# RWKV scan: one 128-row product per head for output and for state, identity and old state added on TensorE

## What is computed

```python
def step(s, inp):
    w_t, k_t, v_t, kk_t, a_t = inp[:5]
    sa = jnp.einsum('bhvk,bhk->bhv', s, kk_t)
    s = (s * w_t[:, :, None, :] - sa[..., None] * (kk_t * a_t)[:, :, None, :]
         + v_t[..., None] * k_t[:, :, None, :])
    if not want_out:
        return s, None
    return s, jnp.einsum('bhvk,bhk->bhv', s, inp[5])
```

## Time and profile before

| | |
|---|---|
| time, median of 3 runs | 2241.44 us (2238.55 to 2246.93) |
| span of the profiled execution | 2243.0 us, of which no time outside the span is given |
| busy in it: PE, DVE, ACT, POOL | 2044.1, 1366.9, 786.2, 275.6 us |
| the scan phase | from 973.9 us; the next phase's chain of work begins at 1277.4 us |
| granted clock of TensorE, mean | 0.954 of 2.4 GHz |

### The profile page before, as it was taken

One profiled execution on the slowest core, in us unless ns is written; L12 is line 12 of the kernel. 1 busy time (PEld: TensorE's weight loads), 2 busy tenths in 40 slices (PEclk: granted clock), 3 DMA queues, 4 the chain that ended last, 5 costly groups with the idle time before them and its releaser, 6 DMA issues. The chain is left out here.

```text
span 2243.0 us, 38706 instructions
## 1 busy us (share of the span) xinstructions
PE 2044.1 (91%) x16787; PEld 1683.7 (75%) x16787; DVE 1366.9 (61%) x1287; ACT 786.2 (35%) x858; POOL 275.6 (12%) x135
## 2 busy tenths in 40 slices
PE   7679999999899989966677799989999999999997
PEld 3258888888678876656666688778888888888886
DVE  3465666665438547758888678366565656554444
ACT  1231112113062225524433365344343434333333
POOL 0242213123104214301000020000000000000000
PEclk9589999999899999988999899999999999999998
DMA  9989888886264368977444287535555555555552
GB/s 327 349 273 335 309 310 301 310 316 193 90 170 106 85 186 262 302 194 189 86 88 88 52 205 269 204 120 188 187 187 187 187 188 188 185 206 188 191 199 98
DMA packets 406153, 454.18 MB, mean 202 GB/s; under 512 B 107551, under 2 KB 356751, under 8 KB 388735
## 3 DMA queue, kind: packets, MB, share of 16 engines
q1 hardware_dynamic: 398400, 441.04, 62.0%
q10 hardware_dynamic: 7614, 11.10, 1.3%
HBM read 413.89 MB, written 38.22 MB: 202 GB/s over the span
## 5 line engine op out<-in xcount | busy, mean ns | idle before, releaser
L215 DVE TENSOR_TENSOR f_w_lo<-t_w_raw,f_w_hi 128x2048 fp32r<-128x2048 f32 x132 | 302.2, 2290 | 308.1 <-ACT f_w_hi L209 308.1
L270 PE MATMUL pf<-h,f_w_hi 128*128 128x512 f32 x1320 | 463.9, 395 | 0.0
L209 ACT ACTIVATE f_w_hi<-t_w_raw 128x2048 fp32r<-128x2048 f32 x132 | 253.2, 1918 | 446.8 <-PE pf L270 283.6
L269 PE MATMUL pf<-h,f_w_lo 128*128 128x256 f32 x1320 | 367.4, 278 | 0.3 <-DVE h L2603 0.3
L270 PEld LDWEIGHTS pf<-h,f_w_hi 128*128 128x128 f32 x1320 | 247.6, 188 | 54.3
L269 PEld LDWEIGHTS pf<-h,f_w_lo 128*128 128x128 f32 x1320 | 248.3, 188 | 4.6 <-DVE h L2603 0.6
L209 ACT ACTIVATE p_w_hi<-h_w_raw 128x2048 fp32r<-128x2048 f32 (+1 forms) x52 | 96.4, 1901 | 340.6 <-DVE stage L726 252.2
L261 PE MATMUL p_in<-h,p_w_lo 128*128 128x512 f32 (+1 forms) x512 | 199.3, 389 | 0.0
L259 PE MATMUL p_in<-h,p_w_hi 128*128 128x512 f32 (+1 forms) x512 | 199.3, 389 | 0.0
L260 PE MATMUL p_in<-h,p_w_hi 128*128 128x512 f32 (+1 forms) x512 | 199.3, 389 | 0.0
L2799 PE MATMUL d_out<-f_w_hi,hid 128*128 128x512 f32 x704 | 178.7, 394 | 6.2 <-DVE f_w_lo L215 6.2
(11 more groups left out here) (417 smaller groups left out, 3362.9 us busy)
## 6 DMA issues: line engine op xcount, KB each, us to landing
h_of_x<-in_ada_w SPq DMA_DIRECT2D x64, 1024.0 KB, 5.1
h_w_raw<-in_w_in SPq DMA_DIRECT2D x51, 1024.0 KB, 7.5
t_w_raw<-in_ffn_w_gate SPq DMA_DIRECT2D x44, 1024.0 KB, 5.1
t_w_raw<-in_ffn_w_up SPq DMA_DIRECT2D x44, 1024.0 KB, 5.1
t_w_raw<-in_ffn_w_down SPq DMA_DIRECT2D x44, 1024.0 KB, 4.9
h_w_raw<-in_ada_w SPq DMA_DIRECT2D x32, 1024.0 KB, 8.8
gate_w<-in_w_in SPq DMA_DIRECT2D x32, 1024.0 KB, 6.2
t_w_raw<-in_w_out SPq DMA_DIRECT2D x16, 1024.0 KB, 5.7
```

The source lines that it names most:

```text
L209: act.activation(self.hi[:, m % self.S, 0:w], self.raw[:, s, 0:w], ACT.Copy)\
L215: eng.tensor_tensor(self.lo[:, m % self.S, 0:w], self.raw[:, s, 0:w], b32(self.hi[:, m % self.S, 0:w]), ALU.subtract)\
L269: pe.matmul(hi, wl, x[:, 0, k, :], start=False, stop=False)
L270: return pe.matmul(both, wh, x[:, :, k, :], start=False, stop=last)
```

## The change

It pairs operands so that a product over 128 rows does what two over 64 did. `uv` holds, for each head, u on one half of the partitions and v on the other; which half is which depends on the parity of j. `r12` holds `r1` and `r2`, `st12` holds `s1t` and `s2t` in the same way, and `s12` (rate and key side by side, in an order that depends on the parity) takes the place of `ldr`'s rows 1 and 2; to have it so, `phase_rwkv_pre` writes keys and rates, and v, of odd pairs in swapped places. Outputs of `uv` are copied from PSUM in two parts, by parity.

Two additions go to TensorE: `inverse` is preceded by a product of identities in f32r (`eye_r`, `eyes_r`), after which `xt` is only 0.5 x PSUM, a copy on ScalarE; and `u_step` puts the old state into PSUM by a product with `eye`, so that VectorE's `state` is the multiplication by `e_end` alone.

```diff
@@ phase_rwkv_pre, store
-                    sp.dma_start(shared_d.rearrange("p (a j) t -> p a j t", a=2)[:, :, j, :], sh[:, j % 3])\
+                    apart = PAIRS + 1 - 2 * b
+                    sp.dma_start(shared_d[:, j:j + apart + 1:apart, :], sh[:, j % 3])\
...
@@ run
-                go("flips2", now)
+                go("halve", lev)
                 if not early:
                     go("prepare", ahead)
                     go("forward", ahead)
-                go("halve", lev)
@@ SyncE
                     if c:
-                        for n in ("q1", "b", "s2tr"):
+                        sp.wait_ge(sm("b", d), c)
+                    sp.dma_start(ld[d][:], dir_d[d, :, 0:U8, at:at + C]).then_inc(sm("in", d), 16)
+                    if c:
+                        for n in ("q1", "strn"):
                             sp.wait_ge(sm(n, d), c)
-                    sp.dma_start(ldr[d][:].rearrange("p a u t -> p (a u) t"), dir_d[d, :, :, at:at + C])\
-                      .then_inc(sm("in", d), 16)
+                    for n in range(2):
+                        sp.dma_start(s12[d][:, :, n, :], dir_d[d, :, U8 + U8 * n:2 * U8 + U8 * n, at:at + C])\
+                          .then_inc(sm("in_s12", d), 16)
@@ VectorE, scores
-                    dve.tensor_tensor(quads(r1[d][:]), narrow(pb[d]), mask(INCL, d), ALU.mult)\
-                       .then_inc(sm("r1", d), 1)
+                    dve.tensor_tensor(r12[d][:], whole(pb[d]), masks[:, d, INCL, :].unsqueeze(1)
+                                      .broadcast_to([P, 2 * U8, C]), ALU.mult).then_inc(sm("r12", d), 1)
@@ VectorE, halve and state
-                    dve.scalar_tensor_tensor(out=quads(xt[d][:]), in0=narrow(pa[d]), scalar=0.5,
-                                             in1=quads(half_eye[:]), op0=ALU.mult, op1=ALU.add)\
-                       .then_inc(sm("inverse", d), 1)
...
-                    dve.tensor_tensor(by_parity(S[d][:]), by_parity(S[d][:]), narrow(pa[d], 1), ALU.add).then_inc(sm("sadd", d), 1)
-                    dve.wait_ge(sm("sadd", d), c + 1)
                     dve.wait_ge(sm("e_end", d), c + 1)
-                    dve.tensor_tensor(S[d][:], S[d][:], e_end[d][:].unsqueeze(2).broadcast_to([P, U8, C]), ALU.mult)\
-                       .then_inc(sm("S", d), 1)
+                    dve.tensor_tensor(by_parity(S[d][:]), narrow(pa[d], 1), e_end[d][:].rearrange("p (u b) -> p b u", b=2)
+                                      .unsqueeze(3).broadcast_to([P, 2, U8 // 2, C]), ALU.mult).then_inc(sm("S", d), 1)
@@ ScalarE
-                    act.activation(quads(vt[d][:]), narrow(pb[d]), ACT.Copy).then_inc(sm("vt", d), 1)
+                    for b in range(2):
+                        act.activation(own_blocks(uv[d], b)[HEAD[1 - b]].rearrange("p h u c -> p u h c"),
+                                       pb[d][HEAD[1 - b], 0:BANK].rearrange("p (u h c) -> p u h c", h=2, c=C), ACT.Copy).then_inc(sm("vt", d), 1)
...
+                    act.activation(st12[d][:], whole(pa[d]), ACT.Copy).then_inc(sm("st12", d), 1)
+
+                def halve(c, d):
+                    act.wait_ge(sm("k", d), c + 1)
+                    act.activation(quads(xt[d][:]), narrow(pa[d]), ACT.Copy, scale=0.5).then_inc(sm("inverse", d), 1)
...
-                    act.activation(quads(u[d][:]), narrow(pa[d]), ACT.Copy).then_inc(sm("uc", d), 1)
+                    for b in range(2):
+                        act.activation(own_blocks(uv[d], b)[HEAD[b]], narrow(pa[d])[HEAD[b]], ACT.Copy).then_inc(sm("uc", d), 1)
@@ TensorE, scores3, tokens, flips
+                    pe.wait_ge(sm("first", d), c + 1)
...
+                        last = pe.matmul(by_block(pb[d], j, h), s12[d][HEAD[h], j].rearrange("p a c -> p (a c)"),
+                                         feat(q12[d][:, :, 1, :], j, h), start=True, stop=True)
...
-                        pe.wait_ge(sm("r1", d), c - 3)
-                    turn_all(pb, kkv[d][:, 1], d).then_inc(sm("vtr", d), 1)
+                        pe.wait_ge(sm("r12", d), c - 3)
...
+                    for j in range(U8):
+                        last = pe.transpose(pa[d][:, j * P:(j + 1) * P], s12[d][:, j].rearrange("p a c -> p (a c)"), eye[:])
+                    last.then_inc(sm("strn", d), 1)
@@ TensorE, grow level 0
-                        pe.wait_ge(sm("s1t", d), c + 1)
+                        pe.wait_ge(sm("st12", d), c + 1)
@@ TensorE, inverse and u_step
+                    for b in range(2):
+                        pe.matmul(pa[d][:, b * BANK:b * BANK + BANK // 2], eye_r[:],
+                                  eyes_r[:].rearrange("p u c -> p (u c)"), start=True, stop=False, skip_group_check=True)
...
+                    goes_on = c != LAST
+                    if goes_on:
+                        for b in range(2):
+                            at = b * BANK + BANK // 2
+                            pe.matmul(pa[d][:, at:at + BANK // 2], eye[:],
+                                      S[d][:].rearrange("p (u b) c -> p b u c", b=2)[:, b], start=True, stop=False,
+                                      skip_group_check=True)
@@ TensorE, output and state
-                        pe.matmul(by_feature(pb[d], j, h), flip(vt[d], j, h), tok(r2[d], j, h), start=False, stop=False, skip_group_check=True)
-                    pe.wait_ge(sm("uc", d), c + 1)
-                    for j, h in UNITS:
-                        last = pe.matmul(by_feature(pb[d], j, h), tok(u[d], j, h), tok(r1[d], j, h), start=False, stop=True, skip_group_check=True)
+                        at = block_of(j, h)
+                        last = pe.matmul(by_feature(pb[d], j, h), uv[d][:, at, :], r12[d][:, at, :], start=False, stop=True,
+                                         skip_group_check=True)
...
+                    for j, h in UNITS:
+                        last = pe.matmul(by_feature(pa[d], j, h, 1), st12[d][:, 2 * j + h, :], uv[d][:, block_of(j, h), :],
+                                         start=False, stop=True, skip_group_check=True)
```

146 lines of the change are left out of this document (66 added, 80 removed).

## The result

The changed kernel takes 2246.48 us (median of 10 runs, 2242.30 to 2252.39) against 2241.48 us before (10 runs on the same chip); the ratio is 1.0029 with a 95% interval of 1.0015 to 1.0042. It got slower, by 5 us between the medians and 6.5 us by the ratio, where 8.6 us less were forecast. The profiled execution has a span of 2246.1 us, so it stands for the median.

What follows compares the result with a forecast made beforehand. VectorE (nearly without holes in context half steps) and, in latent ones, TensorE's instruction supply were taken to bound the kernel; 4.4 (context) + 3.2 (latent) + 1.0 (start) = 8.6 us off 2241.4 gave 2232.8 us, range 2217 to 2249.

Steps and rivals of the forecast that it cites:

- the sum for the latent half step: Latent half step: 18.1 us of chain plus 0.5 us remaining of the supply gaps, 18.6 us instead of 19.0.
- +1.4 us: Latent half step without instruction supply: +0.9 at level 2, +1.2 at level 0, -0.7 for the state addition gone.
- (2): Latent half step: scores3 doubles from 0.5 to 0.93 us plus a 0.1 switch, r12 waits; 0.7 us of level 0's delay.
- VectorE's work, 20 us less: Whole kernel: halving (10.8 us) and state addition (9.5 us) leave VectorE, 20.3 us of busy time.
- Identity ahead of u, +0.9 on level 2: Latent half step: the product of identity and old state takes 1.1 us between level 1 and u; level 2 costs 0.9 more.
- Level 0, 1.2 us later, of which the copies of v make 0.5: Latent half step: level 0 returns 1.2 us later, 0.7 from scores3 and r12, 0.5 from the copies of v.
- Supply: Latent half: instructions arrive one packet per about 4.0 us; 16.1 us per half step against 18, 24 to 25 packets against 27.
- Context half steps, 0.55 us shorter: Context half step: halving gives 0.3 us, state addition 0.5, identity product costs 0.25; 4.4 us over 8.
- The start, 1.0 us: Start of the scan: the smaller load ld lands ahead of s12, gaining 1.0 of the first scan's 1.6 us wait.
- The second one: Rival: the chain grows and the supply gives nothing back, gaps staying as long; +5.8 us, 2247 us, chance 0.15.
- The third: Rival: 128-row products don't overlap, so state and output take up to 3.7 us each; 2280 us, chance 0.10.
- The first: Rival: VectorE's time comes off whole, a gain of 20 us or more; 2220 us, chance 0.20.

Runs made afterwards that it cites:

- e1: Changed kernel with each 64x128 product of scores3 made two 64x64 products on alternating quarters of the array; 2238.95 us, ratio 1.0001 to the kernel before.
- e4: Changed kernel with scores3 in quarters, flips ahead of the tokens, and the carried-state products ahead of level 1; 2230.92 us, ratio 0.9974 to the kernel before.
- e5: Changed kernel with the addition of the old state back on VectorE and the products of identity and state gone; 2247.10 us, ratio 1.0024 to the kernel before.
- e6: Changed kernel with halving and identity again one VectorE operation, f32r identity products and ScalarE's halving gone; 2243.82 us, ratio 1.0018 to the kernel before.
- e3: Changed kernel with the two products of identity and old state moved two steps earlier, behind the sum for rhs; 2242.96 us, ratio 1.0016 to the kernel before.
- e14: Kernel of e13 with the two copies of v also made one, leaving out more of state and output; 2247.85 us, ratio 1.0034 to the kernel before.
- e2: Changed kernel with the flips of the sources and their copy ahead of the tokens and the copies of v; 2247.43 us, ratio 1.0038 to the kernel before.
- e13: Changed kernel with ScalarE's two copies of u made one of 128 partitions, leaving out part of the result; 2247.26 us, ratio 1.0028 to the kernel before.
- e7: Kernel before the change without the r2 by v output products and s2 by v state products, 32 fewer per latent half step; 2221.09 us, ratio 0.9908.
- e9_early_inverse: Kernel of e4 with VectorE's transposes into cross ahead of r12 and the inverse with its halving ahead of the tokens; 2230.84 us, ratio 0.9958.
- e8: Changed kernel with VectorE's two transposes into cross ahead of r12 instead of behind it; 2246.63 us, ratio 1.0022 to the kernel before.
- e11: Kernel before the change with the products that e7 removes kept, but cut to 2 of their 64 columns; 2241.94 us, ratio 1.0010.

## Why the prediction was wrong

**The step that failed** is the sum for the latent half step: "With 18.1 us of chain and 16.1 us of supply I expect 0.5 us of it to remain: 18.6 us". It measured 20.4 us. That is the larger part of the error; a context half step missed by 0.7 us (16.7 for 16.0). Two terms of the latent sum failed.

The first is the chain, "+1.4 us". A clean latent half step of the changed kernel has 14.3 us of VectorE's work and waits of 1.54, 1.49 and 1.35 us, 18.7 us in sum and not 18.1. The mis-sized part is (2), `scores3` "0.5 to 0.93, one switch of 0.1": it went from 0.50 us (1214.47 to 1214.96 before the change) to 1.93, 0.9 us more than I had. e1 brings it to 0.99 and takes 0.8 us off the wait for `r12`.

The second is what remains beside the chain. TensorE's gaps did fall to 0.5 us per half step, but the half step lies 1.7 us above the clean one. Over the six that is 10 us. Of these, 3.5 are waits for `r12` and level 2 behind groups that ran at the granted clock of 0.50 in part or whole (2.90, 2.44 and 2.57 us instead of 1.35, 1.54 and 1.54), 2.7 are such waits where records came late (2.83, 2.07 and 2.08 us), and 2.2 are waits for `first`. I subtracted the relief from the half step as if gaps and TensorE's work were apart. A gap in which instructions arrive can be TensorE's slack; here TensorE filled it with longer work. For this reading stand e4, in which the shorter work brings 10.4 us of gaps back, and the busy time, 13.9 before and 16.4 us after per latent half step. That it is the whole reason isn't shown.

The sentence "TensorE's time is thus unchanged; what falls is the count" holds for the products it speaks of. At full clock the output took 0.47 + 0.47 us and the state, whose two groups are interleaved, 0.93 before the change, 1.87 together; after it 0.95 to 0.98 and 1.03 to 1.06. What the prediction never did is to add up TensorE's time over the whole half step. These lines make up the 14.7 us by which it grew over six:

| us busy | before | after |
|---|---|---|
| scores2 | 9.4 | 5.2 |
| scores3 | 5.1 | 13.3 |
| identity by S | none | 7.7 |
| f32r identity of the inverse | none | 2.9 |

(Busy times of lines can't be added where groups are interleaved, as in the state before the change, so I compare output and state by their starts.)

Point by point:

- *scores3, "0.5 to 0.93, one switch of 0.1".* Measured 1.93 us. I counted 64x128 as two tiles at the pace of a row with two tiles; the timeline gives 1.93 us for 32 records, 0.060 each, and its weight loads of 128 columns last 188 ns where those of 64 last 135. What e1 changes here is worth 6 to 7.5 us of the whole.
- *VectorE's work, 20 us less.* In the profiles 24.1 us less (1366.9 to 1342.8). As traded it was worth nothing: e5 and e6 put it back, half each, with TensorE's products gone, and were no slower.
- *Identity ahead of u, +0.9 on level 2.* Level 2 clean is waited for 1.35 us, 1.06 above before's 0.29. The mechanism and about its size were right (e3, e5); the product itself takes 1.06 us to the start of u, 1.1 forecast.
- *Level 0, 1.2 us later, of which the copies of v make 0.5.* The wait is 1.49 us, 1.3 forecast. The part of the copies was too large: the second copy of v costs 0.2 (e14), not 0.5. By the timeline it is the chain scores3, `r12`, tokens, flips, copy, and with the flips first (e2) 0.6 us of it go.
- *Supply.* 24 packets for 24 to 25, and 3.1 us of gaps in six half steps: right for the gaps, wrong for the half step, as above.
- *Context half steps, 0.55 us shorter.* They are 0.2 us longer in the mean, and the clean ones 14.76 against 14.43 to 14.49, 0.3 longer. The state was to save 0.5 us and waits 0.54 instead, the second of two copies of u ahead of it, which the sum left out; with one copy (e13) that wait goes from four of five half steps, and the whole stays. Level 2 is waited for 0.42 and level 0 0.72 us; I had 0.25 for the one and 0.2 for the other.

```profile
1070.31 0.72 DVE L1485 STREAM_TRANSPOSE turned_b<-pa 128x512 f32<-128x512 f32 x1 [0.72 <-PE pa L1715]
...
1077.24 0.69 DVE L1535 TENSOR_TENSOR S_f<-pa,e_end_f 128x512 f32<-128x512 f32 x1 [0.54 <-PE pa L1788]
```

- *The start, 1.0 us.* Can't be judged: the first copy into `first_f` starts at 982.1 after the change and 986.3 before, but in the ten experiments that change nothing ahead of it, it starts anywhere from 978.2 to 985.3.
- *The rivals.* The second one's 2247 us is what was measured, and that is luck: its chain grew, but the gaps it wanted unchanged fell from 21.5 to 3.1 us, and the 4.4 us that it takes off for the context half steps didn't come. The third is refuted: 128x64 products run at 0.03 us per record. The rule of the Trainium skill ("TensorE: Matmul & The Clock Gate", Part 3, "The mechanism"), by which products that share the row group don't overlap their weight loads, is thus not what these groups show (0.95 to 1.06 us for 32 records whose loads last 138 ns each, 4.4 us if one by one). The same section names the background weight buffer as a second case in which a load is pulled ahead; these groups would fit it, and no run here tests it. The first falls: VectorE is 24 us less busy and the kernel is slower.

What stays open: how much of e7's 20 us is supply and how much TensorE's time, since a product of few columns takes as long; and whether the state could start on half of u (a half of the products writes the bank that ScalarE still reads, so it was not tried).

The best version found is e9_early_inverse: 0.42% below the kernel before (0.9958, 0.9943 to 0.9974) and some 16 us below the changed one. e4_all_three, with three edits, is at the same median and can't be told from it.

## What to carry to other kernels

Taking work off the busiest engine is worth its time only if the engine that hands over to it does not get slower: sum TensorE's own time group by group for the new shapes, and follow it in its fixed order, before counting VectorE's savings. Merging two products into one of a wider shape saves instructions, but its price per product has to be read for that shape; here a 64x128 product took nearly twice as long as the two 64x64 ones that do the same (1.93 against 0.99 us for sixteen). Read it from one group's start to the next, in a window that holds the whole group. And a wait that is filled with other work tells whether it is on the path: where the next wait grows by as much (e8), the chain runs through the other engine. Before a longer wait is put down to an edit, look whether the granted clock was the same behind it.

## What the runs showed of the hardware

- Sixteen 64x128 products with 64 moving columns take 1.93 us; the same work as thirty-two 64x64 products on alternating quarters takes 0.99 us (e1). Sixteen 128x64 products take 0.95 to 1.06 us.
- At a granted clock of 0.50 the same sixteen 64x128 products take 3.60 us instead of 1.93 (e6).
- Two of 64 moving columns instead of all 64 shorten a group of sixteen 64x64 products on four tiles from 0.47 to 0.44 us (e11).
- ScalarE's copy of 64 partitions by 512 columns takes as long as one of 128 partitions (592 against 590 to 597 ns in the same profile):

```profile
L1584 ACT ACTIVATE uv_b<-pb 64x512 f32<-64x512 f32 x16 | 9.5, 592 | 18.0 <-PE pb L1693 17.8
```

- Thirty-two products fewer in a half step of 284 bring four packets fewer in six half steps (27 to 23) and 2 us per half step (e7), which holds both what the instructions and what the products cost.
